# Who starts the loads of the shared modulation chunks: SyncE in its order of weight chunks, or GpSimd as their buffer comes free

## The reference

```python
# first block: 32 experts, 4 per token, d = d_ff = 1024
gu = xe @ w_gate_up[e] + b_gate_up[e]
act = (u + 1.0) * (g * jax.nn.sigmoid(SWIGLU_ALPHA * g))
y = act @ w_down[e] + b_down[e]
...
# second block, for each of its two layers l
mod  = (jax.nn.silu(c) @ ada_w[l] + ada_b[l])[:, None, :]     # ada_w[l]: 1024 x 6144
modc = jax.nn.silu(c_ctx) @ ada_w[l] + ada_b[l]
sh1, sc1, g1, sh2, sc2, g2 = jnp.split(mod, 6, axis=-1)
h = modulate(rms_norm_2(x, mix_pre_g[l]), sh1, sc1)
p = h @ w_in[l]
```

## Time and profile before

| | us |
|---|---|
| median of three runs | 3294.3 |
| the profiled execution | 3297.4 |
| its span, first to last instruction | 3295.5 |
| TensorE busy | 3062.7 (93%) |
| VectorE busy | 1458.0 (44%) |
| ScalarE busy | 484.7 (15%) |
| GpSimd busy | 26.6 (1%), 37 instructions |
| packets of SyncE's queue, share of the 16 DMA engines | 55.8% |

### The profile page before, as it was taken

How to read it: one execution, slowest core, us unless ns; L and a number is a source line. 1 busy time by engine, 2 the same in 40 slices (tenths; PEclk the granted TensorE clock), 3 DMA queues, 4 the chain that set the end, 5 groups by cost and what they waited for, 6 DMA issues and landing times.

```text
span 3295.5 us, 31281 instructions
## 1 busy us (share of the span) xinstructions
PE 3062.7 (93%) x12162; PEld 1767.8 (54%) x12162; DVE 1458.0 (44%) x3449; ACT 484.7 (15%) x972; POOL 26.6 (1%) x37
## 2 busy tenths in 40 slices
PE   5877889998998999999998999989999999999898
PEld 3464224454544454554437757844444487587764
DVE  5754664355776665444422884220000337732201
ACT  1121100012221111010011223111000101321100
POOL 0000000000000000000000000000000000000000
PEclk9857999999999999999998999999999999999999
DMA  8513999897887987899993432312121243223342
GB/s 338 223 52 134 414 412 377 371 370 318 351 352 314 389 351 289 369 382 376 375 384 118 153 128 77 137 69 75 65 89 65 89 154 137 93 97 135 127 153 89
DMA packets 101041, 740.58 MB, mean 225 GB/s; under 512 B 11232, under 2 KB 11616, under 8 KB 12160
## 3 DMA queue, kind: packets, MB, share of 16 engines
q1 hardware_dynamic: 99504, 733.00, 55.8%
q10 hardware_dynamic: 1392, 5.58, 0.5%
HBM read 737.48 MB, written 1.05 MB: 224 GB/s over the span
## 4 chain that ended last, share of the span: by engine, by line
PE 80%; DMA 10%; DVE 6%; ACT 2%; issue 1%; SPq 0%; DVEq 0%; ACTq 0%
PE ps L498 26%; PE ps L510 17%; PE ps L745 10%; PE ps L660 8%; DMA ring<-stream 7%; PE ps L824 4%; PE ps L656 3%; PE ps L772 2%; PE ps L528 2%; PE ps L760 2%; PE ps L752 1%; DVE area L1033 1%; DMA area<-shared_modulation 1%; DMA area<-modulation 1%; PE ps L949 1%
## 5 line engine op out<-in xcount | busy, mean ns | idle before, releaser
L498 PE MATMUL ps<-area,ring 128*128 128x256 f32 (+1 forms) x3456 | 864.0, 412 | 0.3
L498 PEld LDWEIGHTS ps<-area,ring 128*128 128x128 f32 x3456 | 659.9, 191 | 201.9 <-issue 122.9
L510 PE MATMUL ps<-ring,area 128*128 128x512 f32 x1440 | 621.2, 593 | 2.1 <-DMA ring<-stream 2.1
L745 PE MATMUL ps<-ring,area 128*64 128x512 f32 x2112 | 492.0, 613 | 36.2 <-DMA ring<-stream 34.8
L510 PEld LDWEIGHTS ps<-ring,area 128*128 128x128 f32 x1440 | 273.4, 190 | 342.1 <-issue 337.0
L745 PEld LDWEIGHTS ps<-ring,area 128*64 128x64 f32 x2112 | 146.6, 140 | 358.2 <-issue 271.1
L1317 DVE SCALAR_TENSOR_TENSOR area<-area,cond 128x256 f32<-128x256 f32 x672 | 270.1, 481 | 0.0
L660 PE MATMUL ps<-area,ring 128*128 128x256 f32 x1152 | 256.4, 381 | 2.4 <-DMA ring<-stream 1.3
L660 PEld LDWEIGHTS ps<-area,ring 128*128 128x128 f32 x1152 | 216.4, 190 | 44.6 <-issue 16.5
L1839 DVE TENSOR_TENSOR area<-area 128x512 f32<-128x512 f32 (+1 forms) x64 | 35.8, 559 | 460.6 <-ACT area L2216 460.6
L824 PE MATMUL ps<-ring,area 128*64 128x512 f32 x1056 | 233.9, 595 | 4.4 <-ACT area L2058 4.4
(11 more groups left out here) (307 smaller groups left out, 2019.3 us busy)
## 6 DMA issues: line engine op xcount, KB each, us to landing
ring<-stream SPq DMA_DIRECT2D x626, 1024.0 KB, 8.9
area<-shared_modulation SPq DMA_DIRECT2D x48, 1024.0 KB, 7.0
area<-modulation SPq DMA_DIRECT2D x16, 1536.0 KB, 7.8
x<-x_tiles ACTq DMA_DIRECT2D x1, 1024.0 KB, 12.8
area<-ctx_tiles ACTq DMA_DIRECT2D x1, 1024.0 KB, 4.8
out<-x SPq DMA_DIRECT2D x1, 1024.0 KB, 3.9
cst<-constants ACTq DMA_DIRECT2D x1, 928.5 KB, 13.0
rows<-row_vectors ACTq DMA_DIRECT2D x1, 912.0 KB, 9.7
```

What stands on the lines that cost most here:

```text
L498: i = mm(ps[:, b, 0:n], w[:, k % 4, j * P:(j + 1) * P], rhs(k), start=(k == 0), stop=(k == 4 * kgs - 1))
L510: i = mm(ps[:, b, :], lhs(k, t), w[:, k % 4, :], start=(k == 0), stop=(k == 4 * kgs - 1))
L745: i = mm(ps[half(h), bank, :], xT[:, k % 4, half(k // 4)], w[:, 2 * (k % 2) + h, :], start=(k == 0), stop=False)
```

## The change

The 48 loads of shared chunks move from SyncE's order to GpSimd's. GpSimd waits once for the end of the first modulation (`("part", MOD1 - 1)`), whose buffers lie in the same place, and then for each chunk until VectorE has read the one before it. VectorE waits for a semaphore of their own, `shared_landed`. The loads' sizes, source and destination, and the work of all other engines stay as they are.

```diff
--- before.py
+++ after.py
@@ -296,6 +296,7 @@
         K = Signals(nc, ctx, known, per)
         mark, at, last = K.mark, K.at, K.last
         landed = [K.sem(f"weights_landed{s}") for s in range(RING)]
+        shared_landed = K.sem("shared_modulation_landed")
         mods_landed = [K.sem(f"modulation_weights_landed{s}") for s in range(2)]
 
         def v(off, *shape):
@@ -1305,7 +1306,7 @@
                 if at_ not in MOD_AT:
                     return
                 m = MOD_AT.index(at_)
-                dve.wait_ge(mods_landed[0], 16 * (MOD1 // 2 + 1 + m))
+                dve.wait_ge(shared_landed, 16 * (m + 1))
                 for k in range(KD):
                     for s in range(2):
                         c = cond[:, 8 + 8 * s + k:9 + 8 * s + k]
@@ -2231,6 +2232,11 @@
         def _(pool):
             pool.wait_ge(*at("x1"))
             nc.gpsimd.memset(bgu, 0.0).then_inc(*mark("bias_cleared", "bgu_cleared"))
+            pool.wait_ge(*at(("part", MOD1 - 1)))
+            for m in range(LAYERS * MODS):
+                if m:
+                    pool.wait_ge(*at(("part2", m - 1)))
+                pool.dma_start(mods2, mods2_d[m]).then_inc(shared_landed, 16)
             for l in range(LAYERS):
                 N = SEQ
                 L = f"L{l}"
@@ -2269,13 +2275,6 @@
                     load_mod(g)
             sp.wait_ge(*at(("part", MOD1 - 1)))
 
-            def load_mod2(at_):
-                if at_ in MOD_AT:
-                    m = MOD_AT.index(at_)
-                    if m:
-                        sp.wait_ge(*at(("part2", m - 1)))
-                    sp.dma_start(mods2, mods2_d[m]).then_inc(mods_landed[0], 16)
-
             def context(e, place):
                 step = PLACE.get((e, place))
                 if step and place in "AB":
@@ -2285,10 +2284,6 @@
                     sp.wait_ge(*at("flag"))
                     top = nc.sync.value_load(flag[0:1, 1:2], min_val=0, max_val=NE - 1)
                 for ci in range(CPE):
-                    if ci == (2 if e else 0):
-                        load_mod2((e, 0))
-                    if ci == 10:
-                        load_mod2((e, 1))
                     if ci == 4:
                         context(e, "A")
                     if ci == 8:
```

## The result

| | before | changed |
|---|---|---|
| median, us | 3294.0 (4 runs, 3288.8 to 3295.5) | 3272.9 (4 runs, 3270.8 to 3278.0) |
| the profiled execution | 3297.4 | 3274.4 |
| its span | 3295.5 | 3272.5 |
| TensorE busy | 3062.7 | 3049.8 |
| GpSimd busy | 26.6, 37 instructions | 52.0, 85 instructions |

The ratio is 0.9938, with a 95% interval from 0.9923 to 0.9954: the changed kernel is 21 us faster. The forecast was 3265, the range 3256 to 3288. Its sum was 28.9 us, so a quarter of it is missing, and the profile should tell which terms. The gain is clear of the noise, though it is 0.6% of the time.

A forecast was written before the change was run, and what follows sets the result against it. Transfers were taken to bound 320 to 480 us, TensorE 500 to 1640 us. Gains of 3.8 + 4.7 + 9.9 + 7.5 + 3 = 28.9 us, taken from the 3294.3 us median, gave 3265 us, range 3256 to 3288.

The forecast's parts named there:

- The forecast mechanism: Expert blocks: ring loads no longer wait behind shared loads and the DMA engines stay full; 3265 us, chance 0.57.
- the prediction's own signs of being wrong: Shared loads over 10 us in mid-block, a rate under 400 GB/s before 480 us, new waits in up groups.
- Block 23, 9.9 us: Late VectorE holds SyncE; freed, TensorE's 6.96 us wait, 0.38 hidden and 2.5 of clock come back.
- The even bursts, 7.5 us: Gate bursts of even blocks, 500 to 1640 us: shared load done before the burst, so all small waits go.
- The odd bursts, 3 us: Bursts of odd blocks: load starts at most 2.2 us earlier; 40% of the waits taken, ends 0 and 7.4.
- No cost: Shared loads moved among up chunks fit the spare time; 1.2 us left at the tightest odd block, block 7.
- Blocks 0 to 5, 8.5 us: 3.8 us from fuller engines in blocks 0 to 4, plus 4.7 in block 5, including 2.7 of clock.
- The term of blocks 0 to 4, 3.8: Transfer-bound stretch 320 to 480 us: four windows below 424 GB/s, put down to SyncE standing at shared chunks.
- (2): Rival: mixed queues are slower by 0.63 us a load, 13.2 us over 21 loads; 3282 us, chance 0.17.
- (3): Rival: GpSimd's load takes double, 4.9 us of the engines; 3320 us; chance 0.07 with every extra above 1.2 us.
- (4): Rival: bursts unchanged, TensorE's wait passes to the next late chunk; only blocks 5 and 23 gain; 3280 us, chance 0.12.
- (5): Rival: GpSimd reaches its loads late; chance 0.07 shared with a cost near break-even.

The follow-up runs named there:

- unblock_only: Changed kernel, but GpSimd starts each shared load not before the place SyncE's order gave it; 3280.4 us, ratio 0.9963 against before.
- sp_early: Kernel before, SyncE keeping all shared loads; from block 4 on, those of even blocks are issued earlier, out of the bursts before even blocks; 3283.3 us, ratio 0.9973.
- hold_mid: Changed kernel; from block 5 the load freed by a block's first shared step waits until TensorE used the context chunk; 3269.5 us, repeated as `hold_mid_again` 3270.4 us.
- one_load: Changed kernel without 47 of the 48 shared loads, VectorE running the same steps on the first chunk; 3245.5 us, ratio 0.9851 against before.
- hold_all: `hold_mid`, with the load an odd block uses first also held from block 5 until that block's first gate chunk is reached; 3288.1 us, ratio 0.9981.

## Why the prediction was right, and where its sum was off

**The forecast mechanism held**: ring loads are freed and the engines stay full. The time lies in the range, 8 us above the forecast. Averaged over the three traces of the changed kernel, the terms of the sum come to 3.9 us for blocks 0 to 5 (forecast 8.5), 5.4 for the even bursts (7.5), 3.4 for the odd ones (3) and 9.6 for block 23 (9.9), 22.3 in all: the first two hold what is missing. Of the prediction's own signs of being wrong some showed: shared loads of over 10 us in mid-block (up to 10.9), windows under 400 GB/s before 480 us, and a new wait in an up group. They belong to the terms below, not to a rival.

**Block 23, 9.9 us: right.** 9.6 in the three traces of the changed kernel and in `unblock_only`, 8.5 and 8.9 where the load was held; 0.3 in `sp_early`, where SyncE still stood. The working (wait, its hidden 0.38, and 2.5 of clock, 9.8 us when added up) was exact to 0.3.

**The even bursts, 7.5 us: the mechanism right, the changed kernel reaches half of it to nearly all.** `sp_early`, `hold_mid` and `hold_mid_again` show 7.7, 7.5 and 7.6. The changed kernel shows 3.8, 7.2 and 5.1. The step that failed is "GpSimd's load is through long before the burst": true of the block's first chunk, but the prediction did not ask what its early landing sets free. VectorE no longer waits, ends its steps at 603.5 in block 8 and not at 616.4, and so the *second* chunk's load goes out into the burst's tail. The prediction had worked that out for block 14, where VectorE's steps end at 896.1 in the trace of before, with TensorE at its last gate chunk; it took VectorE's times as fixed, though they hung on the loads that the change moved.

**The odd bursts, 3 us: right in size, in part by luck.** 2.8 in the first trace, 1.7 to 5.8 in all; the 40% was a choice, and no run shows that share. A loss is hidden in it that the prediction had ruled out ("No cost"). In block 17 of the changed kernel the load of 1037.89 falls among the up chunks, and one of them is late by 1.25 us (before, the up group of this block had no wait):

```profile
1037.89 0.53 POOL L2239 DMA_DIRECT2D area<-shared_modulation  x1 [16.26 <-DVE area L1318]
```

```profile
1038.62 5.37 PE L746 MATMUL ps<-ring,area 128*64 128x512 f32 x24
1045.24 1.94 PE L746 MATMUL ps<-ring,area 128*64 128x512 f32 x8 [1.25 <-DMA ring<-stream]
```

That was the cover "that a slow load would use up", with 1.2 us left by my working at the tightest place I looked at. Block 17 is tighter, and takes 1.9 us longer than before (0.6 and 2.2 in the other two traces), 0.4 of it in the gate group.

**Blocks 0 to 5, 8.5 us: mis-sized.** The seven traces of kernels with GpSimd's loads of full size in these blocks show 2.9 to 4.8 from block 0 to block 6, nearly all of it in block 5 (3.1 to 4.1 against 4.7). The term of blocks 0 to 4, 3.8, came out between a loss of 1.2 and a gain of 1.7. Two steps failed. The first: rates below 424 in a window were all put down to SyncE. The windows at 330 and 400 still read 395 and 396 GB/s (384 and 396 before), with no wait of SyncE for VectorE left; only those at 440 and 470 rose, to 420 and 418, which is 10 x (23 + 62) / 424 = 2.0 us, and the one at 330 gives 0.3 more. The DMA share, next to last in a row, had it already: two of the windows before, and the one at 330 of the changed kernel:

```profile
400.00:410.00 10.00, 9.14 (x42) 3.00 (x44) 7.42 (x20) 1.07 (x2) 0.00 (x0) 1.00 0.99 396
440.00:450.00 10.00, 6.66 (x30) 1.78 (x26) 4.81 (x14) 0.60 (x1) 0.00 (x0) 1.00 0.97 397
```

```profile
330.00:340.00 10.00, 10.00 (x50) 3.37 (x48) 3.38 (x9) 0.60 (x1) 0.53 (x1) 1.00 1.00 395
```

In the four windows before the engines were idle for 3, 1, 3 and 11% of 10 us, 1.8 us in all, and not 3.8; the rest of the missing rate came with busy engines, from a cause that no run shows. Nor is it shown why the column has still less than 2.3 us. The second: the clock's 2.7 us were added to a stretch whose end the bytes still set. TensorE of the changed kernel, gate's end and the up projection of block 5:

```profile
482.00 1.94 PE L746 MATMUL ps<-ring,area 128*64 128x512 f32 x8 [0.25 <-DMA ring<-stream]
...
486.37 1.94 PE L746 MATMUL ps<-ring,area 128*64 128x512 f32 x8
488.51 1.94 PE L746 MATMUL ps<-ring,area 128*64 128x512 f32 x8 [0.21 <-DMA ring<-stream]
491.01 1.94 PE L746 MATMUL ps<-ring,area 128*64 128x512 f32 x8 [0.56 <-DMA ring<-stream]
493.50 1.94 PE L746 MATMUL ps<-ring,area 128*64 128x512 f32 x8 [0.55 <-DMA ring<-stream]
```

The last three up chunks start 2.5 us apart, the time of their bytes, and not 1.75. The gate group gained 6.1 us (13.45 before, from 478.51 to 491.96; now 7.38, from 476.38 to 483.76), and the up group gave 2.0 back (6.92 before, now 8.89). The transfers are the limit until some 494 us, not 480.

**The rivals.** (2) and (3), a dearer queue: false. The 10 us with a whole GpSimd load among ring loads ran at 420 GB/s, and `one_load` prices a load at 2.3 us, not the 3.1 of (2); a load costs its bytes. (4), nothing in the bursts changes: true for `unblock_only`, which gave its 3280 to 0.4 us, and false for the change. (5): the first load goes out at 267.05, as worked out.

The Trainium skill, DMA: Bandwidth & Descriptors, "Measured (HBM→SBUF, 128 partitions, SWDGE, issued from GpSimd)", gives 341 GB/s for a load of 1 MB. By that figure, an estimate, the result would have been near 3282. The trace does not agree: with a whole load of GpSimd's among ring loads the engines moved 420 GB/s, as the last section shows.

## What to carry to other kernels

A load that waits for another engine doesn't belong in the ordered queue that feeds the bounding engine: on an idle engine's queue its lateness holds up no other load, and that alone was worth 13 of the 21 us. It can still come too late for its own use, as in `hold_all`. When you move a load, follow what its earlier landing sets free, one step further than the wait that you remove: the consumer finishes earlier, and the next load starts at a time that the old trace doesn't show. And where transfers are the limit, price a freed stall by the time that the DMA engines were idle, and not by a rate below the best; TensorE's clock or waits come on top only once the chunks behind it have landed.

## What the runs showed of the hardware

**Two queues share the engines, at nearly no loss of rate.** The transfers of the changed kernel from 440 to 450 us, by queue: packets, MB, share of the 16 engines' time.

```profile
DMA packets 577, 4.20 MB, mean 420 GB/s; under 512 B 64, under 2 KB 64, under 8 KB 64
...
q1 hardware_dynamic: 433, 3.15, 75.7%
q0 software_dynamic: 144, 1.05, 25.2%
```

One GpSimd load (1.05 MB) lies in there whole, at 420 GB/s against the 419 to 425 of the full windows of before. Of the 48 loads of the changed kernel 38 take 9.2 to 10.9 us from issue to landing, with ring loads in flight; eight, issued with at most the end of one in flight, take 5.0 to 5.2 (the other two 6.0 and 7.8). In SyncE's own order the median was 7.0. A load of GpSimd's doesn't stand behind the ring loads in flight: the one issued at 436.63 landed after 9.7 us, at 446.3, and a ring load issued before it, at 435.17, took 13.5 us, to 448.7. But it takes a quarter of the engines' time from them, 25.2% in this window. So a load in the tail of the burst makes the chunk behind it late.

**The clock ahead of block 0.** From 272 to 282 us the granted clock is 0.50 in the trace of before, the lower of TensorE's two levels (1.2 GHz), and 0.76 in that of the changed kernel, at the higher one for about half of the time. TensorE goes through the same steps in both, behind a wait of 5.71 us for VectorE. Before, then changed:

```profile
273.60 6.88 PE L603 MATMUL ps<-area 128*128 128x32 f32 x32
```

```profile
273.35 3.76 PE L604 MATMUL ps<-area 128*128 128x32 f32 x32
276.93 3.56 PE L529 MATMUL ps<-cst,area 128*128 128x128 f32 x16
```

The 32 matmuls take 6.88 us before and 3.76 changed: 3.1 us of the 3.4 that the changed kernel is ahead at block 0. `unblock_only` and `hold_mid` were only 0.3 and 0.6 us ahead there, and the repetition of `hold_mid` 2.9, so it is the execution and not the edit. What decides when the clock rises there stays open. Whoever compares two single traces of this kernel should subtract it first.
